# Dense experts for 336 tokens instead of 342: six more tokens go through gathers

## The chip, the cores and the metric

The kernel runs on one core of a Trainium2 chip. The metric is the device time of an execution in microseconds, as the median of the runs. Beside it there is one profiled execution, whose trace is read here. The core has TensorE (PE, matmuls), VectorE (DVE), ScalarE (ACT), GpSimd (POOL) and SyncE (SP), whose queue issues nearly all plain DMAs; GpSimd issues the gathers.

## The reference

One encoder layer on two groups of 256 tokens of width 2048, 512 tokens in all, in fp32. After norm and modulation comes a mixer (retention and differential attention), and then the part that this change is about, a retrieval of experts:

```python
def _peer(h, w_query, sub_keys, u_tab, v_tab):
    def block(xb):                                  # 128 tokens
        q = (xb @ w_query).reshape(TOKEN_BLOCK, PEER_HEADS, 2, PEER_QDIM // 2)
        s = jnp.einsum("nhpd,hpkd->nhpk", q, sub_keys)
        sv, si = lax.top_k(s, PEER_TOPK)            # 16 of 128 keys, twice
        ...                                         # 16 best pairs of 256, per head
        g = jax.nn.softmax(top_s, axis=-1)          # 8 x 16 = 128 slots a token
        hid = jax.nn.gelu(jnp.einsum("nd,ned->ne", xb, u_tab[eidx]))
        return jnp.einsum("ne,ned->nd", g * hid, v_tab[eidx])
```

There are 128 x 128 = 16384 experts, each one row of 2048 in `u_tab` and one in `v_tab`. Each token uses 128 of them. The layer ends with a norm, a gate and the residual.

## The kernel before

The first 1230 us hold the modulation, the projections, the mixer and its output product, and the routing (which 128 experts each token takes, with which gates). The change leaves them nearly as they are. Then two ways of computing the experts run side by side.

**Dense.** For `ND` = 342 of the 512 tokens (tokens 128 to 469) every expert is computed and weighted with a table of gates that is zero where a token does not use an expert. The experts go in 128 blocks of 128. An *up unit* is one block of `u`, 1 MB: 48 matmuls with 128 columns of weights stationary and 342 token columns moving, in fp32 split in a high and a low part (hi x hi and hi x lo on L1096, low x hi on L1103). ScalarE makes the high part of the weights (`raw_hi`, L1504), VectorE the low part (`raw_lo`, L2082); then ScalarE does gelu, VectorE multiplies by the gates (`up_gate`), and the product is split again into `w_hi` and `w_lo`. A *down unit* is 1 MB of `v`, 8 blocks of it by 256 output columns: 48 matmuls (L1157, L1158, L1163) into two PSUM banks, which VectorE adds to `y_t` (`y_add`, L2203). Eight ups and eight downs are a super block; `ORDER` lists all 256 units, unit k in place k. SP loads unit k + 3 once unit k is done, into a ring of three.

**The gate table.** It is made before the dense loop settles, in the *table stage*: for each dense token a product of two one-hot matrices (L1138), in groups of four tokens, between the products of seven up units (`TABLE_UNITS`). VectorE and ScalarE make the one-hots, ScalarE moves the results to a stage buffer of 38 tokens (`table_out`), and SP stores it to DRAM when full. Nine stages make 342. The last one is stored in four quarters, so that the first blocks can be loaded early. In the dense loop SP loads the gates of four blocks at a time (`g_load`) into `g_ring`.

**Gathered.** Token rows 0 to 127 (one per partition, 128 slots each) and the last 42 tokens (*mixed*, three partitions for each token, 43 slots each) fetch only the rows that they use: 171 gathers of u rows, one row of 8 KB for each partition, each followed by a dot product on VectorE (`dot`, L2212) in phase one, and 171 gathers of v rows with a multiply-add into `acc_a` or `acc_x` on VectorE (`accumulate`, L2225) in phase two. The ring has three buffers, and GpSimd issues gather n when dot n - 3 is done. `GATHERS[k]` says which dots VectorE does in its step k, the step in which it also serves units k - 1 and k + 1: phase one at steps 17 to 132, phase two at 137 to 254. At `TURN` the hidden values go through gelu and get their gates. At the end TensorE adds `acc_x` to its 42 tokens by a matmul with the 0/1 matrix `pick_x`.

Order on an engine is the order of the code; semaphores tie the engines.

Of the kernel before, what the change touches and what calls it, by code (L numbers as in the profile page):

```python
# [69 lines left out]
ND = T - P - XT  # L70
# [8 lines left out]
DOTS = SLOTS + XSLOTS  # L79
# [6 lines left out]
STAGE = 38  # L86
# [51 lines left out]

def slot_at(n):
    m, j = n // 4, n % 4  # L140
    return (False, SLOTS + m) if j == 1 else (True, 3 * m + max(j - 1, 0))
# [11 lines left out]
def build_program(nc, x, ct, c_rows, ada_w, ada_wt, ada_b, rows, w_t, w_v, w_o, w_q, keys_t, decay, lams, post1, pre2, post2,  # L153
                  u_t, v_t, u_tab, v_tab, ident_c, dist_c, alibi_c, iota_c, out, mod_d, silu_d, mix_d, g_d, x1_d):
# [8 lines left out]
    with ExitStack() as ctx:  # L163
# [107 lines left out]
        acc_x = placed("acc_x", W0, [P, D])[:, :]  # L271
        h2_hi = rounded("h2_hi", W0 + LOOP, [P, KD, ND])
# [6 lines left out]
        eidx_last = take(SLOTS).bitcast(u32)  # L279
# [17 lines left out]
        stage = [placed(f"stage{n}", a, [P, NKEYS, STAGE]) for n, a in enumerate((M0, at))]  # L297
# [74 lines left out]
        def bank(i):  # L372
            return psum[:, i * NB:(i + 1) * NB]
# [69 lines left out]
        def _(sp):  # L443
# [219 lines left out]
            def stage_store(n, quarters=(0,)):  # L663
                sp.wait_ge(S["g_ev"], PER_STAGE * (n + 1))
                if n < NSTAGE - 1:
                    sp.dma_start(g_d[n], stage[n % 2][:, :, :].rearrange("p i c -> p (i c)")).then_inc(S[f"g_out{n % 2}"], 16)
                    return

                for q in quarters:
                    i = slice(QUARTERS[q], QUARTERS[q + 1])  # L670
                    sp.dma_start(g_d[n, :, i.start * STAGE:i.stop * STAGE], stage[n % 2][:, i, :].rearrange("p i c -> p (i c)"))\
                        .then_inc(S[f"g_quarter{q}"], 16)

            def g_load(q):
# [4 lines left out]
                sp.dma_start(g_ring[:, q % 2, :, :], g_d[:, :, QUAD * q * STAGE:QUAD * (q + 1) * STAGE].rearrange("n j c -> j n c"))\  # L679
# [10 lines left out]
            for a in range(XG):  # L690
# [18 lines left out]
            for k in range(EARLY - 1, UNITS):  # L709
# [1781 lines left out]
```

## Time and profile before

| | us |
|---|---|
| median of 3 runs | 3285.76 (3284.59 to 3288.32) |
| the profiled execution, its own time | 3282.5 |
| its span in the trace | 3280.7 |
| TensorE busy | 3218.1 (98%) |
| VectorE busy | 2664.5 (81%) |
| ScalarE busy | 1044.9 (32%) |
| GpSimd busy | 924.3 (28%) |
| DMA | 914 MB, 279 GB/s over the span |

Busy times of matmuls overlap, since they are pipelined: what a matmul costs is read from the start of one to the start of the next. Idle time of an engine that is not the bottleneck costs nothing. Line numbers are those of the kernel before.

### The profile page before, as it was taken

The numbers are of one execution on the slowest core, as the hardware profiler recorded it, in microseconds if no ns is written. First come the engines' busy times: TensorE is split into PE (matmuls) and PEld (weight loads), VectorE is DVE, ScalarE is ACT, GpSimd is POOL, SyncE is SP. The second block draws the span as 40 slices with busy tenths as digits, with TensorE's granted clock in tenths as the row PEclk, the third lists the DMA queues.
The fourth block names the chain that finished last, engine by engine and source line by source line (L and its number), as shares of the span: only waits on it lengthen the run. The fifth ranks groups of instructions, "written<-read, shape, count | busy, mean of one in ns | idle before, by whom it ended". The sixth has DMA issues, their size and how long they took to land. (4 is left out here: it accounts for less than half of the span.)

```text
span 3280.7 us, 48326 instructions
## 1 busy us (share of the span) xinstructions
PE 3218.1 (98%) x19393; PEld 2969.5 (91%) x19393; DVE 2664.5 (81%) x3913; ACT 1044.9 (32%) x1380; POOL 924.3 (28%) x542
## 2 busy tenths in 40 slices
PE   7999999998999999999999999999999999999998
PEld 3788888888995449999999999999999999999998
DVE  4688888887885769968888888888688888888888
ACT  2222323234222005943323332332332332323332
POOL 2100000003551775013333333333133332343332
PEclk9999999999999999999999999999999999999999
DMA  9845444445556103579999999999799989999987
GB/s 393 310 161 176 161 167 170 169 161 200 204 196 266 72 32 122 223 267 370 348 361 358 356 355 364 354 348 363 292 370 351 361 345 348 356 351 353 360 336 294
DMA packets 174222, 914.05 MB, mean 279 GB/s; under 512 B 16303, under 2 KB 54104, under 8 KB 79832
## 3 DMA queue, kind: packets, MB, share of 16 engines
q1 hardware_dynamic: 124790, 552.84, 45.4%
q0 software_dynamic: 49248, 358.63, 28.0%
q8 instruction: 130, 2.13, 0.3%
q14 instruction: 54, 0.44, 0.0%
HBM read 875.79 MB, written 34.03 MB: 277 GB/s over the span
## 5 line engine op out<-in xcount | busy, mean ns | idle before, releaser
L1504 ACT ACTIVATE sb_raw_hi<-sb_raw_ring 128x2048 fp32r<-128x2048 f32 x256 | 491.0, 1918 | 1144.9 <-DMA sb_raw_ring<-in_v_t 559.6
L2082 DVE TENSOR_TENSOR sb_raw_lo<-sb_raw_ring,sb_raw_hi 128x2048 fp32r<-128x2048 f32 x256 | 586.0, 2289 | 107.5 <-ACT sb_raw_hi L1504 107.1
L1096 PE MATMUL ps_all<-sb_h_hi,sb_raw_hi 128*128 128x342 f32 x2048 | 646.0, 320 | 0.0
L1096 PE MATMUL ps_all<-sb_h_lo,sb_raw_hi 128*128 128x342 f32 x2048 | 645.6, 320 | 0.0
L1157 PE MATMUL ps_all<-sb_w_hi,sb_raw_hi 128*128 128x342 f32 x2032 | 639.7, 319 | 5.1 <-DVE sb_w_lo L2187 3.6
L1158 PE MATMUL ps_all<-sb_w_lo,sb_raw_hi 128*128 128x342 f32 x2032 | 639.0, 320 | 0.0
L2409 POOL DMA_INDIRECT sb_gather_ring<-in_u_tab,sb_kept x171 | 298.6, 1746 | 742.5 <-DVE sb_kept L2212 564.3
L2409 POOL DMA_INDIRECT sb_gather_ring<-in_v_tab,sb_kept x171 | 306.0, 1789 | 615.7 <-DVE sb_acc_a L2225 410.0
L1157 PEld LDWEIGHTS ps_all<-sb_w_hi,sb_raw_hi 128*128 128x128 f32 x2032 | 385.2, 190 | 7.0 <-issue 4.3
L1096 PEld LDWEIGHTS ps_all<-sb_h_lo,sb_raw_hi 128*128 128x128 f32 x2048 | 386.0, 188 | 0.0
L1096 PEld LDWEIGHTS ps_all<-sb_h_hi,sb_raw_hi 128*128 128x128 f32 x2048 | 385.4, 188 | 0.0
L1158 PEld LDWEIGHTS ps_all<-sb_w_lo,sb_raw_hi 128*128 128x128 f32 x2032 | 383.5, 189 | 0.0
L1103 PE MATMUL ps_all<-sb_h_hi,sb_raw_lo 128*128 128x342 f32 x2048 | 352.0, 321 | 0.5 <-DVE sb_raw_lo L2082 0.5
L1163 PE MATMUL ps_all<-sb_w_hi,sb_raw_lo 128*128 128x342 f32 x2032 | 340.2, 319 | 0.0
L1103 PEld LDWEIGHTS ps_all<-sb_h_hi,sb_raw_lo 128*128 128x128 f32 x2048 | 326.0, 189 | 1.0 <-DVE sb_raw_lo L2082 1.0
L1163 PEld LDWEIGHTS ps_all<-sb_w_hi,sb_raw_lo 128*128 128x128 f32 x2032 | 323.8, 188 | 0.0
L2225 DVE SCALAR_TENSOR_TENSOR sb_acc_a<-sb_gather_ring,sb_kept,sb_acc_a 128x2048 f32<-128x2048 f32 x127 | 298.2, 2348 | 12.4 <-DMA sb_gather_ring<-in_v_tab,sb_kept 9.0
L2335 POOL TENSOR_TENSOR sb_w_low<-sb_w_raw,sb_w_high 128x1024 fp32r<-128x1024 f32 (+1 forms) x36 | 92.4, 2594 | 744.9 <-ACT sb_w_high L1433 744.9
L2212 DVE CUSTOM_DVE_ANT_0 sb_gather_ring<-sb_gather_ring,sb_arena 128x2048 f32<-128x2048 f32 x128 | 290.9, 2287 | 2.9 <-DMA sb_gather_ring<-in_u_tab,sb_kept 2.8
L1305 ACT ACTIVATE sb_w_high<-sb_w_raw 128x1536 fp32r<-128x1536 f32 (+1 forms) x62 | 104.9, 1694 | 370.5 <-PE ps_all L773 367.2
L771 PE MATMUL ps_all<-sb_h_hi,sb_w_high 128*128 128x512 f32 x480 | 191.7, 399 | 2.1 <-DVE sb_h_lo L1709 1.7
L772 PE MATMUL ps_all<-sb_h_lo,sb_w_high 128*128 128x512 f32 x480 | 187.1, 390 | 0.0
(325 smaller groups left out, 5268.3 us busy)
## 6 DMA issues: line engine op xcount, KB each, us to landing
sb_raw_ring<-in_u_t SPq DMA_DIRECT2D x128, 1024.0 KB, 6.9
sb_raw_ring<-in_v_t SPq DMA_DIRECT2D x128, 1024.0 KB, 7.2
sb_arena<-in_ada_wt SPq DMA_DIRECT2D x94, 512.0 KB, 6.0
sb_w_raw<-in_w_t SPq DMA_DIRECT2D x32, 1024.0 KB, 4.9
sb_small<-in_ada_w SPq DMA_DIRECT2D x30, 1024.0 KB, 11.2
sb_w_raw<-in_w_v SPq DMA_DIRECT2D x32, 768.0 KB, 4.4
sb_g_ring<-table_scratch SPq DMA_DIRECT2D x32, 684.0 KB, 9.8
table_scratch<-sb_stage SPq DMA_DIRECT2D x8, 2432.0 KB, 8.2
```

Source lines behind the costliest of these rows:

```text
L771: mm(b, a_hi, b_hi, start=start, stop=False)
L772: mm(b, a_hi, b_lo, start=False, stop=False)
L1096: last = mm(acc, raw_hi[:, r[0], kk * P:(kk + 1) * P], part[:, kk, :], start=i == 0, stop=False)
L1103: last = mm(acc, raw_lo[:, place, kk * P:(kk + 1) * P], h2_hi[:, kk, :], start=False, stop=kk == KD - 1)
L1157: mm(accs[c], v, w_hi[:, slots[e], :], start=e == 0, stop=False)
L1158: last = mm(accs[c], v, w_lo[:, slots[e], :], start=False, stop=False)
L1163: last = mm(accs[c], raw_lo[:, place, e * VW + c * P:e * VW + (c + 1) * P], w_hi[:, slots[e], :], start=False, stop=e == S8 - 1)
L1504: acti(raw_hi[:, k % 2, :], raw_ring[:, k % RAW, :], ACT.Copy).then_inc(S["un_hi"], 1)
L2082: vec.tensor_tensor(raw_lo[:, k % RAW, :], raw_ring[:, k % RAW, :], raw_hi[:, k % 2, :].bitcast(f32), ALU.subtract)\
L2212: vec.tensor_tensor_reduce(out=ring, in0=ring, in1=h2a if own else h2x[rows, :], scale=1.0, scalar=0.0, op0=ALU.mult, op1=ALU.add, accum_o ...
L2225: vec.scalar_tensor_tensor(acc, ring, hid_all[rows, c:c + 1], acc, ALU.mult, ALU.add).then_inc(S["gr_used"], 1)
L2409: pool.indirect_dma_start(out=gather_ring[:, n % GRING, :], out_offset=None, in_=u_tab if n < DOTS else v_tab, in_offset=bass.IndirectOffs ...
```

## The change

Six of the dense tokens (464 to 469) become a third kind of gathered token, *few*: 21 partitions for each token, 6 x 21 = 126 partitions, 7 slots in each. That makes 7 gathers more in each phase, 178 for 171. In phase one they come last, in phase two first. `ND` is 336, the table has 8 stages of 42 tokens, and its DRAM tensor is laid out by expert row, group of four blocks, stage and token, so that a `g_load` reads 5376 bytes in a piece, where it read 608; the stores write pieces of 672 bytes, where they wrote whole rows.

The new tokens' normed rows go to DRAM (`few_d`) and come back near the end of phase one, each spread over 21 partitions, into the place of the mixed tokens' rows, and their expert numbers and gates go by way of `route_d`. Their accumulator lies in that same place, and is folded by TensorE at the start of block 10 into 16 x 6 columns, which are copied into `y_last` at the end.

```diff
+XB = 6
+XBP = P // XB
+XBR = XB * XBP
+ND = T - P - XT - XB
+XBSLOTS = -(-SLOTS // XBP)
+DOTS = SLOTS + XSLOTS + XBSLOTS
-STAGE = 38
+STAGE = 42
...
+MIXED, FEW = mixed_columns(), list(range(SLOTS + XSLOTS, DOTS))
+COLUMNS = (MIXED + FEW, FEW + MIXED)
+FOLD_BLOCK = 10
...
+        XE_MIXED = 32 * (XG + 1)
+        XE_ALL = XE_MIXED + 32 * XB * len(FEW_PARTS)
...
-                    sp.dma_start(g_d[n], stage[n % 2][:, :, :].rearrange("p i c -> p (i c)")).then_inc(S[f"g_out{n % 2}"], 16)
+                    sp.dma_start(g_d[:, :, n, :], stage[n % 2][:, :, :].rearrange("p (q i) c -> p q (i c)", i=QUAD))\
+                        .then_inc(S[f"g_out{n % 2}"], 16)
...
-                sp.dma_start(g_ring[:, q % 2, :, :], g_d[:, :, QUAD * q * STAGE:QUAD * (q + 1) * STAGE].rearrange("n j c -> j n c"))\
+                sp.dma_start(g_ring[:, q % 2, :, :], g_d[:, q, :, :])\
                     .then_inc(S[f"g_in{q % 2}"], 16)
...
+            sp.dma_start(route_d[0], eidx_last_f[P - XT - XB:P - XT, :]).then_inc(S["xe_in"], 16)
+            sp.dma_start(route_d[1], gates[P - XT - XB:P - XT, NT - 1, :]).then_inc(S["xe_in"], 16)
             next_load(PRE - 1)
+            sp.wait_ge(S["xe_in"], XE_MIXED)
+            for v, dst in enumerate((eidx_x_f, gates_x)):
+                for j in range(XB):
+                    for first, rows_, columns in FEW_PARTS:
...
+                if k == RELOAD:
+                    sp.wait_ge(S["gr_used"], LAST_MIXED + 1)
+                    for j in range(XB):
+                        sp.dma_start(h2x[j * XBP:(j + 1) * XBP, :], few_d[j:j + 1, :].partition_broadcast(XBP)).then_inc(S["h2x_in"], 16)
...
+            def fold_few():
+
+                pe.wait_ge(S["pick_x"], 1)
+                pe.wait_ge(S["gr_used"], DOTS + XBSLOTS)
+                for k in range(KD):
+                    last = mm(bank(2)[:, k * XB:(k + 1) * XB], acc_few[0:XBR, k * P:(k + 1) * P], pick_few[0:XBR, :], start=True, stop=True)
+                last.then_inc(S["yt_done"], 1)
...
-            act.wait_ge(S["xe_in"], 32 * XG)
+            act.wait_ge(S["xe_in"], XE_MIXED)
             for n in range(NGROUP):
```

SP's queue where the table stage begins, before, from the five weight loads ahead of it to the second stage store (`sb_kept` takes the mixed tokens' expert numbers and gates):

```order
L635 DMA sb_raw_ring<-in_u_t 128x2048 x5
L693 DMA sb_kept<-sb_route_a 42x43
L694 DMA sb_kept<-sb_route_b 42x43
L693 DMA sb_kept<-sb_route_a 42x43
L694 DMA sb_kept<-sb_route_b 42x43
L693 DMA sb_kept<-sb_route_a 42x42
L694 DMA sb_kept<-sb_route_b 42x42
L635 DMA sb_raw_ring<-in_u_t 128x2048
L666 DMA table_scratch<-sb_stage_91 128x4864
L635 DMA sb_raw_ring<-in_u_t 128x2048
```

And with the change, from the last of those copies on:

```order
L732 DMA sb_kept<-sb_route_b 42x42
L733 DMA route_scratch<-sb_route_a 6x128
L734 DMA route_scratch<-sb_route_b 6x128
L671 DMA sb_raw_ring<-in_u_t 128x2048
L741 DMA sb_kept<-route_scratch 18x7
L741 DMA sb_kept<-route_scratch 1x2
...
L741 DMA sb_kept<-route_scratch 1x2
L703 DMA table_scratch<-sb_stage_91 4096x1x168
L671 DMA sb_raw_ring<-in_u_t 128x2048
```

Two writes to DRAM stand behind the six copies, ahead of what ScalarE waits for, and 24 small reads stand between a weight load and the first stage store.

VectorE at the end of the loop, before, from the `memset` of `y_last` to the last addition to `y_t` but one:

```order
L2281 MEMSET sb_y_last 128x16x42
L2203 TENSOR_TENSOR sb_y_t<-ps_all,sb_y_t 128x684
L2082 TENSOR_TENSOR sb_raw_lo<-sb_raw_ring,sb_raw_hi 128x2048
L2225 SCALAR_TENSOR_TENSOR sb_acc_a<-sb_gather_ring,sb_kept,sb_acc_a 128x2048
L2225 SCALAR_TENSOR_TENSOR sb_acc_x<-sb_gather_ring,sb_kept,sb_acc_x 126x2048
...
L2203 TENSOR_TENSOR sb_y_t<-ps_all,sb_y_t 128x684
L2082 TENSOR_TENSOR sb_raw_lo<-sb_raw_ring,sb_raw_hi 128x2048
L2225 SCALAR_TENSOR_TENSOR sb_acc_x<-sb_gather_ring,sb_kept,sb_acc_x 126x2048
L2203 TENSOR_TENSOR sb_y_t<-ps_all,sb_y_t 128x684
L2082 TENSOR_TENSOR sb_raw_lo<-sb_raw_ring,sb_raw_hi 128x2048
L2225 SCALAR_TENSOR_TENSOR sb_acc_a<-sb_gather_ring,sb_kept,sb_acc_a 128x2048
L2203 TENSOR_TENSOR sb_y_t<-ps_all,sb_y_t 128x684
```

And with the change, the last two steps of these:

```order
L2272 TENSOR_TENSOR sb_y_t<-ps_all,sb_y_t 128x672
L2150 TENSOR_TENSOR sb_raw_lo<-sb_raw_ring,sb_raw_hi 128x2048
L2296 SCALAR_TENSOR_TENSOR sb_acc_a<-sb_gather_ring,sb_kept,sb_acc_a 128x2048 x2
L2272 TENSOR_TENSOR sb_y_t<-ps_all,sb_y_t 128x672
L2150 TENSOR_TENSOR sb_raw_lo<-sb_raw_ring,sb_raw_hi 128x2048
L2296 SCALAR_TENSOR_TENSOR sb_acc_a<-sb_gather_ring,sb_kept,sb_acc_a 128x2048
L2272 TENSOR_TENSOR sb_y_t<-ps_all,sb_y_t 128x672
```

The last step but one has two accumulates where it had one.

TensorE at the fold, with the change, between the last down unit of block 9 and the first up unit of block 10 (`sb_h2x` holds the few tokens' sums):

```order
L1211 MATMUL ps_all<-sb_w_lo,sb_raw_hi 128x336
L1216 MATMUL ps_all<-sb_w_hi,sb_raw_lo 128x336 x16
L1290 MATMUL ps_all<-sb_kept,sb_h2x 128x6 x16
L1149 MATMUL ps_all<-sb_h_hi,sb_raw_hi 128x336
L1149 MATMUL ps_all<-sb_h_lo,sb_raw_hi 128x336
```

Before, the row of 128x6 is not there, and the others have 342 columns.

## Rows read from the trace of the kernel before

**Rows 1.** Busy time by stretch: length, busy us (instructions), PEclk, DMA share, GB/s.

```profile
1438.30:1442.00 3.70, 3.67 (x13) 3.70 (x14) 2.29 (x1) 0.85 (x1) 3.40 (x2) 0.50 1.07 373
1442.00:1446.00 4.00, 4.00 (x23) 4.00 (x22) 0.00 (x0) 0.00 (x0) 1.24 (x2) 0.80 1.02 425
1800.00:2100.00 300.00, 300.00 (x1912) 300.00 (x1911) 250.29 (x216) 92.06 (x79) 104.58 (x60) 1.00 0.93 356
```

**Rows 2.** The page's memory traffic in 40 equal slices of 82 us.

```profile
GB/s 393 310 161 176 161 167 170 169 161 200 204 196 266 72 32 122 223 267 370 348 361 358 356 355 364 354 348 363 292 370 351 361 345 348 356 351 353 360 336 294
```

**Rows 3.** What TensorE waited for: us in total, times, longest us.

```profile
PE ps_all L1157 <- DVE sb_w_lo L2187: 3.6, 1, 3.6
PE ps_all L1138 <- DVE sb_hot L2166: 3.1, 7, 1.2
PE ps_all L1157 <- ACT sb_raw_hi L1504: 1.2, 3, 0.5
```

**Rows 4.** The page's costliest groups: operands, xcount | busy, mean ns | idle.

```profile
L1096 PE MATMUL ps_all<-sb_h_hi,sb_raw_hi 128*128 128x342 f32 x2048 | 646.0, 320 | 0.0
L1157 PE MATMUL ps_all<-sb_w_hi,sb_raw_hi 128*128 128x342 f32 x2032 | 639.7, 319 | 5.1 <-DVE sb_w_lo L2187 3.6
L2225 DVE SCALAR_TENSOR_TENSOR sb_acc_a<-sb_gather_ring,sb_kept,sb_acc_a 128x2048 f32<-128x2048 f32 x127 | 298.2, 2348 | 12.4 <-DMA sb_gather_ring<-in_v_tab,sb_kept 9.0
```

**Rows 5.** Timeline of TensorE, ends of three unbroken runs: start us, us, what.

```profile
879.74 0.28 PE L772 MATMUL ps_all<-sb_w_low,sb_mix_hi 128*128 128x256 f32 x1
...
899.90 0.28 PE L772 MATMUL ps_all<-sb_w_low,sb_mix_hi 128*128 128x256 f32 x1
...
499.67 0.33 PE L771 MATMUL ps_all<-sb_w_high,sb_h_hi 128*128 128x384 f32 x1
...
509.38 0.34 PE L773 MATMUL ps_all<-sb_w_high,sb_h_lo 128*128 128x384 f32 x1
...
549.93 0.40 PE L772 MATMUL ps_all<-sb_h_lo,sb_w_high 128*128 128x512 f32 x1
...
560.36 0.40 PE L773 MATMUL ps_all<-sb_h_hi,sb_w_low 128*128 128x512 f32 x1
```

**Rows 6.** Timeline of TensorE where the first down unit begins.

```profile
1438.75 0.49 PE L1158 MATMUL ps_all<-sb_w_lo,sb_raw_hi 128*128 128x342 f32 x1
...
1443.31 0.46 PE L1158 MATMUL ps_all<-sb_w_lo,sb_raw_hi 128*128 128x342 f32 x1
```

**Rows 7.** Timelines where the table stage begins: SP's queue, ScalarE, TensorE.

```profile
1283.81 0.75 SPq L694 DMA_DIRECT2D sb_kept<-sb_route_b  x1
...
1301.75 0.33 SPq L666 DMA_DIRECT2D table_scratch<-sb_stage  x1
...
1286.94 0.40 ACT L1562 ACTIVATE sb_hot<-sb_iota,sb_by_slot 128x128 f32<-128x128 f32 x1 [3.00 <-DMA sb_kept<-sb_route_b]
...
1288.01 1.13 PE L1138 MATMUL ps_all<-sb_hot 128*128 128x128 f32 x8 [1.46 <-ACT sb_hot L1564]
```

**Rows 8.** TensorE's table products: ns min/median/max, first and last start.

```profile
L1138 PE MATMUL ps_all<-sb_hot x684: 270/275/378, 1283.4 to 1418.7; 128*128 128x128 f32 x171
```

**Rows 9.** Timelines between table stage and first down unit: SP's queue, VectorE.

```profile
1425.80 1.05 SPq L679 DMA_DIRECT2D sb_g_ring<-table_scratch  x2
...
1430.29 1.79 DVE L2183 TENSOR_TENSOR sb_acc_a<-sb_acc_a,sb_g_ring 128x342 f32<-128x342 f32 x4 [1.13 <-DMA sb_g_ring<-table_scratch]
```

**Rows 10.** Timeline of TensorE: the nearest rows to a matmul of six columns.

```profile
27.96 1.05 PE L758 MATMUL ps_all<-sb_tiny,sb_tops 128*128 128x2 f32 x8 [0.73 <-ACT sb_tops L1272]
```

**Rows 11.** Gathers, line 2409: time from issue to landing.

```profile
DMA to landing us min/median/max: 5.5/9.2/14.1
```

**Rows 12.** Timeline of VectorE at the end of the program.

```profile
3251.52 2.35 DVE L2225 SCALAR_TENSOR_TENSOR sb_acc_a<-sb_gather_ring,sb_kept,sb_acc_a 128x2048 f32<-128x2048 f32 x1
...
3259.86 1.22 DVE L2241 TENSOR_TENSOR sb_raw_ring<-ps_all,sb_gate_sb 128x1024 f32<-128x1024 f32 x1
...
3261.98 0.87 DVE L2203 TENSOR_TENSOR sb_y_t<-ps_all,sb_y_t 128x684 f32<-128x684 f32 x1 [0.90 <-PE ps_all L1163]
```

More of the change, by code:

```diff
@@ L136, in slot_of, with mixed_columns, kind_of @@
     return slots_of(b // S8 % 3)[b % S8]
+def mixed_columns():
+    at = {1 + 15 * m // 4: SLOTS + m for m in range(XSLOTS)}
+    own = iter(range(SLOTS))
+    return [at[n] if n in at else next(own) for n in range(SLOTS + XSLOTS)]
+MIXED, FEW = mixed_columns(), list(range(SLOTS + XSLOTS, DOTS))
+COLUMNS = (MIXED + FEW, FEW + MIXED)
+LAST_MIXED = max(n for n in range(DOTS) if SLOTS <= COLUMNS[0][n] < SLOTS + XSLOTS)
+RELOAD = DOT0 + LAST_MIXED * (TURN - 1 - DOT0) // DOTS + 2
+FOLD_BLOCK = 10
+FOLDED = 1 + 2 * S8 * FOLD_BLOCK + 3
+def kind_of(c):
+    return "own" if c < SLOTS else "mixed" if c < SLOTS + XSLOTS else "few"
 def slot_at(n):
-    m, j = n // 4, n % 4
-    return (False, SLOTS + m) if j == 1 else (True, 3 * m + max(j - 1, 0))
+    c = COLUMNS[n // DOTS][n % DOTS]
+    return kind_of(c), c
 def full_groups(n):
@@ L271, in build_program @@
         acc_x = placed("acc_x", W0, [P, D])[:, :]
+        acc_few = h2x
+        acc_of = {"own": (acc_a, P), "mixed": (acc_x, XP), "few": (acc_few, XBR)}
         h2_hi = rounded("h2_hi", W0 + LOOP, [P, KD, ND])
@@ L296, in build_program @@
         early_w = placed("early_w", at + WR, [P, S8 + 2, ND])
-        stage = [placed(f"stage{n}", a, [P, NKEYS, STAGE]) for n, a in enumerate((M0, at))]
+        stage = [placed(f"stage{n}", a, [P, NKEYS, STAGE]) for n, a in enumerate((at, M0))]
         pick_x = placed("pick_x", at + 2 * WR, [P, P])[:, :]
@@ L1606, in _ @@
                     acti(hid_all[:, 0:SLOTS], hid_all[:, 0:SLOTS], ACT.Gelu)
-                    acti(hid_all[0:XP, SLOTS:DOTS], hid_all[0:XP, SLOTS:DOTS], ACT.Gelu).then_inc(S["hid_gelu"], 1)
+                    for rows_, c in ((XP, slice(SLOTS, SLOTS + XSLOTS)), (XBR, slice(SLOTS + XSLOTS, DOTS))):
+                        last = acti(hid_all[0:rows_, c], hid_all[0:rows_, c], ACT.Gelu)
+                    last.then_inc(S["hid_gelu"], 1)
+                if k == FOLDED:
+                    act.wait_ge(S["yt_done"], 1)
+                    acti(y_few, bank(2)[:, 0:KD * XB].rearrange("p (k j) -> p k j", k=KD), ACT.Copy).then_inc(S["y_last"], 1)
             def y_square(t, half):
                 i = 2 * t - 2 + half
-                act.wait_ge(S["yt_done"], i + 1)
+                act.wait_ge(S["yt_done"], i + 2)
                 c = slice(half * PIECE, (half + 1) * PIECE)
```

85 lines of the change are left out of this document (55 added, 30 removed).

## The prediction

> **What bounds the kernel now.** I read the busy time by stretch first. In the dense stage (about 1440 to 3260 us) TensorE is busy without a gap: 300 us of 300, 1912 matmul records, at the full clock, 1.00, of its two levels, 2.4 GHz [rows 1]. That is 300 / 1912 = 156.9 ns from one matmul of 342 columns to the next. VectorE is busy 250 us of the same 300, the DMA engines 0.93 of it, moving 356 GB/s. Then the waits: of 3280.7 us TensorE waited 3.6 us for the first down unit's `w_lo`, 3.1 us in the table stage and 1.2 us for `raw_hi` [rows 3]. So the time of the dense stage is the number of matmuls times their spacing, and a term counts if it changes either, or if it makes TensorE wait at one of four places: the start of the table stage, the first down unit, a ring that runs late, the tail.
>
> **The narrower matmul.** There are 2048 matmuls on each of three operand pairs of the up units and 2032 on each of three of the down units, as the two rows shown of the six [rows 4], and 48 on the lines of the last block's first down unit, L1186 to L1190: 12288. Seven units (336 matmuls) run inside the table stage and go with it below; 11952 are left. All go from 342 to 336 columns. What six columns are worth comes from the spacing of other widths in this trace, each in a run without a gap. At 256 columns it is 168 matmuls from 879.74 to 899.90 us, 120.0 ns; at 384, 56 matmuls from 499.67 to 509.38, 173.4 ns; at 512, 46 matmuls from 549.93 to 560.36, 226.7 ns [rows 5]. These lie on one line: 53.4 ns for each 128 columns, 0.417 ns a column, and 13.3 ns beside it. The line gives 155.9 ns at 342 columns, but the row gives 156.9: this width pays 1.0 ns that the three others don't. 342 is the only one of the four widths that isn't a multiple of 16, and 336 is one; whether the extra goes with that, no row shows. So the saving is 6 x 0.417 = 2.5 ns a matmul if it stays and 3.5 ns if it goes: 29.9 to 41.8 us. I take 3.2 ns, nearer to the line, since three widths of three lie on it: **38.2 us saved**.
>
> The trace also shows what a lower clock does: with the clock granted at 0.50 (1.2 GHz) [rows 1], the matmuls from 1438.75 to 1443.31 us, 16 spacings, are 285.0 ns apart [rows 6], which is 342 / 1.2 and nothing beside it. The Trainium skill says the same in "TensorE: Matmul & The Clock Gate", section "Wait — 56ns, not 53.3ns?": columns over 1.2 GHz when slow, columns over 2.4 GHz plus a constant when fast. By that rule the 13.3 ns is a constant and nothing is special about 342, so it makes the saving 2.5 ns and the sum 8.3 us later than mine; the 1.0 ns off the line speaks against it, and its constant, about 2.5 ns, is not what these rows show.
>
> **Seven more gathers a phase.** They bring 7 dots and 7 accumulates on VectorE, at 2.35 us for an accumulate [rows 4] and near the same for a dot: 33 us in all, against 50 us idle per 300 us. Per unit VectorE has 178/116 = 1.53 instead of 171/116 = 1.47 of them in phase one. The busy share goes from 0.83 to about 0.88 as the unit shrinks from 7.53 to 7.38 us. Hidden by VectorE's idle time; without that cover it would be the whole 33 us. A gather lands 9.2 us after issue (14.1 at worst) [rows 11], and its ring of three gives it three dots' time, 3 x 4.8 = 14.4 us less one dot. Where two steps with two dots now stand in a row (eight times in phase one, never before) the gap is only some 7.4 us, so VectorE waits 2 us there, and catches up in the next step with one dot. Taken at 0, 0 to +8.
>
> **The fold.** TensorE gets 16 fp32 matmuls of six columns at the start of block 10. The nearest rows are the 128x2 matmuls: 8 records in 1.05 us, some 0.10 us each, two records a matmul [rows 10]. 32 records make **+3.2 us**, 1.6 if both passes overlap, 4.2 if each takes what the first does. Its inputs (accumulates placed some 20 units earlier) are long ready, so it waits for nothing. The copies that follow (ScalarE, VectorE, one DMA) are small and beside it.
>
> **The start of the table stage.** ScalarE waited 3.00 us here for the last copies of route data, and TensorE 1.46 us for ScalarE [rows 7]. The change puts two more DMAs, writes to DRAM, in front of that wait, each at 0.75 us of issue as the one at 1283.81: 1.5 us later. VectorE, which paces the stage, gets its banks later by the same. I take **+1.3 us**, 0.5 if the write lands faster than the copies do, +6 if the longer idle lets the clock fall as it did after 3.6 us at the first down unit. Behind it SP issues 24 small DMAs, 8 to 18 us of queue (0.33 to 0.75 us each), past a unit load whose data is due 40 us later and the first stage store, which was issued at 1301.75 and would now go at 1297 to 1307; ScalarE needs it landed two stages after the start, near 1320. Hidden; nothing.
>
> **The table stage.** It takes 1283.4 to 1418.7 us for 342 tokens [rows 8], 0.396 us each; six fewer make 2.4 us, its share of narrow matmuls included. 88 groups instead of 90, but the half groups cost more per token: **-2.0 us**, -3 to 0.
>
> **The first down unit.** TensorE waited 3.6 us: the stage's first quarter is stored, the two `g_ring` loads go out at 1425.80, VectorE's first gate follows at 1430.29 after waiting for them [rows 9]. Each load was 9 x 128 pieces of 608 B, and is 128 of 5376 B; the store becomes 512 pieces of 672 B for 128 of 2432 B. I give the loads back 1.5 us of their 4.5, the store takes 0.4 more, and the units ahead, shorter by 0.3 us, put TensorE there sooner. Wait 2.8 us, and a little less slow clock behind it: **-1.3 us**. Ends: -6 (no wait, and the 17 slow matmuls at 285 instead of 157 ns gone), +1.
>
> **The tail.** The last step but one has two accumulates instead of one, 2.35 us later on VectorE. Its idle before the last `y` addition is 0.90 us [rows 12]; the rest, **+1.5 us**, reaches the turns, squares and outputs. 0 to +3.
>
> Sum: -38.2 + 3.2 + 1.3 - 2.0 - 1.3 + 1.5 = **-35.5 us**. The profiled execution took 3282.5 us, giving 3247.0; the median of the runs, 3285.76, is 3.3 us above it, giving 3250.3. I say **3249 us**.
>
> **Rivals.**
> *The extra 1.0 ns stays* (2.5 ns a matmul): 8.3 us less saved, **3257 us**. For it: a per-matmul cost needn't know the width. Against: three widths on a line.
> *The DMA engines become the bound.* A unit moves 1.049 MB of weights, 1.474 gathers of 1.049 MB and an eighth of a 0.70 MB gate load, 2.68 MB in 7.53 us, which is the 356 GB/s of the row. After: 2.74 MB in 7.38 us, 372 GB/s. If 356 were the limit, a unit would take 7.70 us, 0.17 more than now, over 234 units with gathers: +40 us where 38 were to be saved, with the small terms about nothing: **3325 us**, slower. It decides from the point where unit loads land so late that ScalarE's `raw_hi` comes after TensorE asks. For it: 0.93 busy. Against: the 356 is just TensorE's demand, slices of 82 us reach 370 GB/s in the dense stage and 393 at the start [rows 2], 4 us reached 425 [rows 1], and some 34000 pieces of 608 B leave the stage (the small pieces are now the table stage's stores). The Trainium skill, "DMA: Bandwidth & Descriptors", section "Specifications", sets about 358 GB/s for a core's HBM traffic; by that rule the rival would come out at 3316 us. The trace doesn't agree: 370 and 393 are above it [rows 2].
> *VectorE falls behind* at the doubled steps and TensorE waits a unit's `w_lo` or bank now and then, 1 us at ten places: **3259 us**.
> *The table stage stalls* on its own stores: 4096 pieces of 672 B a stage. The g_ring loads moved 2304 pieces in 4.5 us, so 8 us of the 16.6 there are. If they took 20, six stages pay 3.5 us: **3270 us**.
> That the change doesn't do what it says has no room: widths and counts are in the program's order.
>
> **How the numbers follow.** Forecast 0.58, extra stays 0.24, VectorE 0.05, stores 0.06, DMA bound 0.07. The likeliest one's own range, with its bounds, is 3238 to 3260. 8 in 10 takes in the second and third and most of the fourth: **3237 to 3268**. What measurement tells from no change is 0.2%, 6.6 us, so faster is below 3279: 0.58 + 0.24 + 0.05 + most of 0.06, set down a little: 0.90. Slower by as much is the DMA case: 0.07. Same: 0.03.
>
> **What would show it.** Right: 153.3 to 153.7 ns a matmul (1953 or so in 300 us), TensorE still 300 of 300, VectorE near 265, DMA near 370 GB/s, the wait for `w_lo` at the first down unit under 3.6 us, the ScalarE wait at the table stage 4 to 5 us, 16 matmuls of six columns in about 3 us. Wrong: 154.4 ns (the extra stayed), TensorE waits for `raw_hi` or `raw_lo` through the dense stage with a DMA behind them, or a table stage longer than 136 us.

## The result

| | before | after |
|---|---|---|
| median of 4 runs each, on one chip, us | 3286.86 (3284.59 to 3288.32) | 3265.84 (3264.57 to 3270.59) |
| the profiled execution, its own time | 3282.5 | 3265.75 |
| its span | 3280.7 | 3263.6 |

The ratio is 0.9938, with a 95% interval of 0.9923 to 0.9953: faster by 0.6%, 21 us. The profiled executions differ by 16.75 us. The forecast was 3249 us, from a gain of 35.5 us, in a range of 3237 to 3268. The sign and the range held, the second by 2 us. Of the gain 21 us came, 16.75 in the profiled executions.

### The profile page after: what moved, and what is told of

The parts are those of the page before. It is cut to its first block and busy times, and to the rows that moved or that the text cites. A ratio compares the mean times of both kernels' runs of the same rounds, so it can differ in the third digit from the quotient of the medians.

```text
span 3263.6 us, 48433 instructions
## 1 busy us (share of the span) xinstructions
PE 3184.7 (98%) x19413; PEld 2936.4 (90%) x19413; DVE 2689.8 (82%) x3930; ACT 1039.4 (32%) x1378; POOL 899.1 (28%) x556
## 5 line engine op out<-in xcount | busy, mean ns | idle before, releaser
L1210 PE MATMUL ps_all<-sb_w_hi,sb_raw_hi 128*128 128x336 f32 x2032 | 627.5, 318 | 19.2 <-ACT sb_raw_hi L1567 15.8
L1149 PE MATMUL ps_all<-sb_h_hi,sb_raw_hi 128*128 128x336 f32 x2048 | 637.4, 318 | 0.0
L1149 PE MATMUL ps_all<-sb_h_lo,sb_raw_hi 128*128 128x336 f32 x2048 | 637.2, 318 | 0.0
L1211 PE MATMUL ps_all<-sb_w_lo,sb_raw_hi 128*128 128x336 f32 x2032 | 626.6, 317 | 0.0
L2486 POOL DMA_INDIRECT sb_gather_ring<-in_u_tab,sb_kept x178 | 283.0, 1590 | 754.3 <-DVE sb_kept L2283 584.9
L2486 POOL DMA_INDIRECT sb_gather_ring<-in_v_tab,sb_kept x178 | 296.7, 1667 | 610.7 <-DVE sb_acc_a L2296 376.0
L1156 PE MATMUL ps_all<-sb_h_hi,sb_raw_lo 128*128 128x336 f32 x2048 | 342.9, 317 | 1.1 <-DVE sb_raw_lo L2150 1.0
L1216 PE MATMUL ps_all<-sb_w_hi,sb_raw_lo 128*128 128x336 f32 x2032 | 333.7, 316 | 0.0
L1156 PEld LDWEIGHTS ps_all<-sb_h_hi,sb_raw_lo 128*128 128x128 f32 x2048 | 319.2, 188 | 1.6 <-DVE sb_raw_lo L2150 1.6
L1216 PEld LDWEIGHTS ps_all<-sb_w_hi,sb_raw_lo 128*128 128x128 f32 x2032 | 316.8, 188 | 0.0
```

Of the source, the lines that this page charges most:

```text
L1149: last = mm(acc, raw_hi[:, r[0], kk * P:(kk + 1) * P], part[:, kk, :], start=i == 0, stop=False)
L1156: last = mm(acc, raw_lo[:, place, kk * P:(kk + 1) * P], h2_hi[:, kk, :], start=False, stop=kk == KD - 1)
L1210: mm(accs[c], v, w_hi[:, slots[e], :], start=e == 0, stop=False)
L1211: last = mm(accs[c], v, w_lo[:, slots[e], :], start=False, stop=False)
L1216: last = mm(accs[c], raw_lo[:, place, e * VW + c * P:e * VW + (c + 1) * P], w_hi[:, slots[e], :], start=False, stop=e == S8 - 1)
L2486: pool.indirect_dma_start(out=gather_ring[:, n % GRING, :], out_offset=None, in_=u_tab if n < DOTS else v_tab, in_offset=bass.IndirectOffs ...
```

## The profile after

First the busy time by stretch (length, busy us of PE, PEld, DVE, ACT and POOL with their instructions, PEclk, DMA share, GB/s), the row that answers to the last of [rows 1], and the page's traffic in 40 slices, which answers to [rows 2]:

```profile
1800.00:2100.00 300.00, 300.00 (x1952) 300.00 (x1951) 262.39 (x226) 97.01 (x86) 91.54 (x61) 1.00 0.96 372
...
GB/s 386 313 168 175 163 164 176 155 177 201 194 193 284 65 39 79 235 265 377 367 375 374 365 380 377 368 374 319 296 379 374 354 369 361 374 364 359 378 361 308
```

300 / 1952 = 153.7 ns from matmul to matmul (156.9 before), VectorE 262 us of 300, 372 GB/s: the steady state is what was forecast. Now TensorE's waits (us in total, times, longest), the rows that answer to [rows 3]:

```profile
PE ps_all L1210 <- ACT sb_raw_hi L1567: 15.8, 3, 12.4
...
PE ps_all L1191 <- ACT sb_hot L1627: 3.2, 2, 1.9
...
PE ps_all L1210 <- DVE sb_w_lo L2256: 2.7, 1, 2.7
...
PE ps_all L1227 <- DVE sb_y_t L2272: 2.0, 1, 2.0
...
PE ps_all L1191 <- DVE sb_hot L2234: 1.4, 3, 0.5
```

The wait for `raw_hi` has grown from 1.2 to 15.8 us, and 12.4 of it is one wait. The timelines of SP's queue, ScalarE and TensorE (start us, duration, what, idle before and its end) show where:

```profile
2232.13 2.03 SPq L766 DMA_DIRECT2D sb_h2x<-few_scratch  x6
2239.12 0.36 SPq L671 DMA_DIRECT2D sb_raw_ring<-in_v_t  x1
...
2264.21 1.91 ACT L1567 ACTIVATE sb_raw_hi<-sb_raw_ring 128x2048 fp32r<-128x2048 f32 x1 [21.70 <-DMA sb_raw_ring<-in_v_t]
...
2266.17 0.65 PE L1210 MATMUL ps_all<-sb_w_hi,sb_raw_hi 128*128 128x336 f32 x1 [12.38 <-ACT sb_raw_hi L1567]
```

This is the reload: six copies of 168 KB, each of which puts one row of `few_d` into 21 partitions of `h2x`. The unit load that SP issues 7 us behind them lands 25 us after its issue, at 2264.19, so late that ScalarE idles 21.7 us and TensorE 12.4. The DMA engines over 2225 to 2275 us, in 40 slices of 1.25 us (busy tenths, GB/s):

```profile
DMA  9999999999989999999999999999999844440099
GB/s 413 406 415 419 433 426 419 406 426 426 387 275 308 269 269 301 301 243 288 216 229 223 282 229 256 288 321 413 419 419 426 374 203 184 184 177 13 0 197 393
```

From 2239 us on they are as busy as ever and move 216 to 321 GB/s instead of 387 to 433, for 20 us; then, near 2266 us, four slices run at full speed on four tenths of the engines (184 GB/s). The stretches around:

```profile
2240.00:2260.00 20.00, 13.79 (x91) 13.51 (x89) 9.62 (x9) 1.92 (x1) 2.80 (x3) 0.96 1.02 277
2260.00:2280.00 20.00, 13.83 (x73) 13.83 (x74) 13.85 (x11) 5.74 (x3) 4.52 (x3) 0.70 0.63 242
2534.00:2538.00 4.00, 4.00 (x37) 4.00 (x35) 3.51 (x3) 1.91 (x1) 2.94 (x2) 1.00 0.62 217
2538.00:2542.00 4.00, 4.00 (x17) 4.00 (x18) 3.01 (x2) 0.00 (x0) 0.72 (x1) 0.57 1.01 428
```

In the second row the granted clock is down to 0.70: after the wait, some 20 matmuls came at the lower of the two levels, 280 ns apart, 2.8 us more; 12.5 + 2.8 is **15.3 us** for the reload. The last two rows are the fold at the start of block 10 and what follows: TensorE has no gap there, but behind its tiny matmuls the clock is 0.57 for 4 us. The fold's own row (ns min/median/max, first and last start) and the second place with a new wait, near the first down unit:

```profile
L1290 PE MATMUL ps_all<-sb_kept,sb_h2x x32: 171/254/254, 2534.6 to 2538.0; 126*128 126x6 f32 x32
```
```profile
1425.45 9.55 SPq L709 DMA_DIRECT2D table_scratch<-sb_stage  x3
1435.05 2.67 SPq L717 DMA_DIRECT2D sb_g_ring<-table_scratch  x1
1437.76 0.45 SPq L671 DMA_DIRECT2D sb_raw_ring<-in_v_t  x1
...
1435.13 0.39 PE L1210 MATMUL ps_all<-sb_w_hi,sb_raw_hi 128*128 128x336 f32 x1 [2.71 <-DVE sb_w_lo L2256]
...
1454.92 0.42 PE L1210 MATMUL ps_all<-sb_w_hi,sb_raw_hi 128*128 128x336 f32 x1 [3.29 <-ACT sb_raw_hi L1567]
```

The first down unit starts at 1435.13 (1438.33 before) after 2.71 us of waiting (3.64 before), but two units on there are 3.3 us of waiting, with slow matmuls behind, 5.1 us together, which before had not.

## The experiments

Ratios are to the kernel before on the same chip; their intervals are about 0.0015 either way, 5 us (from 0.0009 to 0.0025). Smaller differences are read from the traces, by two numbers for each. The *loss* is the time from the first product of the first down unit to the first transposition of `y_t`, which holds 240 units of 48 matmuls, less 11520 times the spacing of that kernel (156.9 ns for the two kernels of 342 columns, 154.2 for the kernel of 336 of 342, 153.7 for the others). The last column is the part of it that falls at the reload: the time between 2230 and 2300 us beyond what its matmuls take at the steady spacing. Both come from one profiled execution each, and a kernel's executions differ by up to 20 us, so the table sets its own time beside the median of its runs: a loss from a profile 9 us below the median, as that of the eight copies, is too small for its kernel. The kernels without the reload, with other rows in it (*own rows*, 126, 128 and 16 rows) and the two narrow ones leave work out or compute with other data; only their times are read.

| kernel | ratio (interval) | profiled / median, us | first down unit, us | first transposition, us | loss, us | at the reload, us |
|---|---|---|---|---|---|---|
| before | 1 | 3282.50 / 3286.86 | 1438.33 | 3252.95 | 7.1 | 0 |
| after | 0.9938 (0.9923 to 0.9953) | 3265.75 / 3265.84 | 1435.13 | 3234.87 | 29.1 | 15.1 |
| no reload | 0.9894 (0.9880 to 0.9908) | 3248.63 / 3251.84 | 1434.73 | 3218.97 | 13.6 | 0 |
| reload in one copy of 126, few rows | 0.9939 (0.9926 to 0.9953) | 3262.21 / 3266.67 | 1435.63 | 3232.54 | 26.3 | 9.1 |
| reload in six copies, rows of their own | 0.9950 (0.9937 to 0.9964) | 3274.60 / 3274.07 | 1438.54 | 3244.39 | 35.2 | 18.6 |
| reload spread over six units | 0.9904 (0.9891 to 0.9917) | 3260.32 / 3257.42 | 1435.00 | 3230.57 | 25.0 | 2.6 |
| reload in one copy of 126 rows | 0.9927 (0.9914 to 0.9941) | 3261.11 / 3261.00 | 1436.26 | 3231.37 | 24.5 | 4.7 |
| reload in one copy of 128 rows | 0.9904 (0.9884 to 0.9924) | 3255.12 / 3253.84 | 1440.11 | 3224.49 | 13.8 | 0 |
| reload in eight copies of 16 rows | 0.9938 (0.9924 to 0.9951) | 3254.37 / 3262.99 | 1436.40 | 3224.55 | 17.5 | 5.5 |
| before, 336 dense tokens alone | 0.9898 (0.9878 to 0.9918) | 3255.98 / 3251.84 | 1435.32 | 3226.61 | 20.7 | 0 |
| before, 336 of 342 columns | 0.9938 (0.9913 to 0.9962) | 3269.39 / 3263.60 | 1438.61 | 3239.94 | 24.9 | 0 |
| after, old layout of the table | 0.9978 (0.9966 to 0.9991) | 3275.00 / 3277.29 | 1436.42 | 3245.34 | 38.3 | 18.4 |
| before, new layout of the table | 1.0012 (1.0003 to 1.0021) | 3290.60 / 3288.94 | 1444.90 | 3261.05 | 8.7 | 0 |
| reload by way of 128 rows, fold spread | 0.9925 (0.9911 to 0.9938) | 3258.09 / 3258.09 | 1439.95 | 3228.40 | 17.8 | 0 |

**What the reload costs.** The theory was that it holds up the load behind it.

```diff
-                if k == RELOAD:
-                    sp.wait_ge(S["gr_used"], LAST_MIXED + 1)
-                    for j in range(XB):
-                        sp.dma_start(h2x[j * XBP:(j + 1) * XBP, :], few_d[j:j + 1, :].partition_broadcast(XBP))...
```

> The changed kernel without the six copies that reload h2x at unit 121; the dots of the six tokens then multiply by the rows that h2x held before, which costs the same time. Theory A (the reload holds up the unit load behind it): the 21.7 us wait of ScalarE for sb_raw_ring and the 12.4 us wait of TensorE for sb_raw_hi near 2264 us go, and with them the slow matmuls behind, so 15 us: about 3250.5 us. Rival B (the transfers of that stretch are late anyway, since the gathers fill the queues): the wait moves by a few us only, 3260 to 3266 us.

The wait is gone, the loss falls by 15.5 us and the ratio by 0.0044, 14.5 us. (Another wait for `raw_hi`, 4.2 us at the second unit behind the first down unit, stays as in after.) Theory A holds: the reload is worth nearly all that the forecast missed.

**Why it costs so much.** Three theories: the six copies lie on a part of the DMA queues and pile up there (1); any burst of 1 MB ahead of a load costs this (2); many reads of one row in DRAM are slow (3). Three edits of the same lines:

```diff
+ one copy:     sp.dma_start(h2x[0:XBR, :], few_d.unsqueeze(1).broadcast_to([XB, XBP, D]))
+ own rows:     sp.dma_start(h2x[j * XBP:(j + 1) * XBP, :], x1_d[j * XBP:(j + 1) * XBP, :])     # six times
+ spread:       if RELOAD <= k < RELOAD + XB: ...                                               # copy k - RELOAD alone
```

> The reload as one DMA over 126 partitions from the same six rows, each read 21 times. Theory 1 (a copy into 21 partitions lies on a part of the 16 queues, and six of them pile up on the same ones): a single copy is spread evenly, it adds 1 MB / 0.37 MB per us = 2.8 us of transfers, the wait of TensorE falls from 12.4 us to 0 to 3 us: 3251 to 3255 us. Theory 2 (1 MB in a burst ahead of a load) and theory 3 (one DRAM row read by all is slow): no change, 3263 to 3267 us.

> The reload still as six DMAs of 21 partitions, but each partition reads a row of its own (of x1_scratch: other data, so the dots of the six tokens are of other vectors). Theory 3 (many reads of one DRAM row are slow): the wait of TensorE falls to 0 to 3 us, 3251 to 3255 us. Theories 1 and 2 (uneven queues, burst): no change, 3263 to 3267 us.

> The six DMAs of the reload go out one per unit, behind the loads of units 124 to 129, instead of all behind that of 124. Theory 2 (the burst): 168 KB is 0.45 us at 372 GB/s, the loads have over 3 us to spare at each unit, so the wait goes: 3251 to 3254 us. Theory 1 (uneven queues): each copy delays its own queues by 21 rows on 7 queues = 3 x 0.31 = about 1 us, hidden as well, 3251 to 3254 us. Theory 3 (slow row): every copy is as slow as before but apart from the others, so the waits are small and repeated, 3254 to 3262 us.

Rows of their own made it no better (TensorE waited 15.9 us): theory 3 is out. One copy of 126 partitions still cost a wait of 6.5 us, 9.1 us with the slow matmuls behind it, and its median of 3266.67 us did not fall below that of after: it came out where theories 2 and 3 had put it, and theory 1 by itself is not enough. Spread over six units the copies cost no wait above 1.7 us and 2.6 us in all; this version was 0.9904 against 0.9938. Its 3257.42 us miss the 3251 to 3254 of theories 1 and 2. The loss of 25.0 is from the slowest but one of its five runs (3260.32 us; they go from 3251 to 3260), and 13 us of it lie behind 2300 us, 7 at the fold and the rest in small gaps, whose cause stays open.

**126 or 128 partitions.** In the slow cases all 16 engines are busy at some 270 GB/s: 0.49 us for 8 KB on each, where 420 GB/s are 0.31. So it isn't only that some queues are longer than others. Theory 4 is that a copy whose partitions are not the 128 of a load is dealt to the queues in another way than the loads, and slows the packets of all. The next kernels differ by two rows.

```diff
+ 126:   sp.dma_start(h2x[0:XBR, :], x1_d[0:XBR, :])
+ 128:   sp.dma_start(h2x, x1_d[0:P, :])
+ 8x16:  sp.dma_start(h2x[j * 16:(j + 1) * 16, :], x1_d[j * 16:(j + 1) * 16, :])     # eight times
```

> The reload as one DMA into all 128 partitions, from 128 rows of x1_scratch (other data for the six tokens' dots). Six copies of 21 partitions and one of 126 both slowed every packet from 0.31 to 0.5 us for over 12 us. Theory 4 (126 or 21 partitions are dealt to the queues unlike the 128 of a load, so that queues write each other's partitions): packets stay at 0.31 us, the rate at 400 GB/s, TensorE waits 0 to 3 us: 3252 to 3256 us. Theory 2 (any burst of 1 MB just there): as the copy over 126, TensorE waits about 6.5 us, 3262 to 3268 us.

> As the run with one copy of 128 rows of x1_scratch, but 126 rows: two rows fewer, the same source, place and moment. Theory 4 (a copy whose partitions are not all 128 is dealt to the queues unlike the loads and the gathers, and slows all packets): rate 190 to 300 GB/s for over 10 us, TensorE waits 5 to 8 us, 3261 to 3267 us. Rival (it was the broadcast from few rows that was slow in the one-copy run, and the six pieces in the other): packets at full speed, 3252 to 3256 us.

> The reload as eight copies of 16 partitions (rows of x1_scratch), 128 in all. If it is the number of partitions over the whole that matters, or that pieces start at a multiple of 16: full speed, 3252 to 3256 us. If every copy of less than 128 partitions is dealt unevenly, as the 21 of each in the changed kernel: TensorE waits about 12 to 16 us, 3264 to 3274 us.

The same 50 us and 40 slices of the DMA engines as above, first for 128 rows in one copy:

```profile
DMA  9999999999999999999999999898999989999998
GB/s 433 426 419 438 419 415 419 439 419 419 419 426 419 426 374 387 406 419 419 426 433 419 393 387 367 334 380 301 328 301 387 334 315 426 360 419 419 426 400 360
```

then for 126 rows in one copy:

```profile
DMA  9999999999999999999999999999999999899598
GB/s 419 413 433 410 427 421 440 413 419 426 426 426 413 413 315 288 315 282 262 256 229 275 315 419 419 419 419 419 419 426 419 419 400 374 262 341 400 138 380 367
```

and for eight copies of 16:

```profile
DMA  9999999999999999999999999999478958989989
GB/s 441 413 430 426 433 433 419 334 210 203 229 243 288 360 406 374 419 419 426 426 426 419 419 419 426 419 413 387 157 131 321 393 118 367 380 236 426 315 321 413
```

With 128 rows the rate stays at 374 to 439 GB/s for 30 us (single slices fall to 301 later), TensorE does not wait, and the loss is that of the kernel without a reload, 13.8 against 13.6. With two rows fewer it sinks to 229 to 315 for nine slices, 11 us, all engines busy. The load behind it is late, TensorE waits 3.1 us, where 5 to 8 were expected, and 4.7 us go in all. The rest of that kernel's loss of 24.5 is not at the reload, and by the runs' times alone the two kernels are not told apart: their intervals overlap. Eight pieces of 16 sink the rate to 203 to 288 for five slices, 6 us, and cost 5.5 us. There TensorE waited for VectorE and not for a load:

```profile
PE ps_all L1210 <- DVE sb_y_t L2272: 4.0, 1, 4.0
```

VectorE had itself waited 4.5 and 2.7 us for two late gathers, in front of the addition to `y_t` that frees the bank. The profile is that kernel's fastest execution; its median, 3262.99 us, lies in neither of the two ranges of the expectation, and nearer to the upper one. So theory 4 holds by the rates and waits of the traces, and its rival form failed: it is not enough that pieces start at a multiple of 16, or that they make 128 in all. Theory 2 stands for nothing by itself: a burst of 1 MB costs nothing here if it is laid out as the loads are. One copy of 126 partitions cost 9.1 us from six rows and 4.7 from 126 rows; whether the source adds something, one execution of each does not decide.

The Trainium skill, "DMA: Bandwidth & Descriptors", section "Why a DMA increments its semaphore by 16 and not by 1", says that a DMA uses the largest number of engines up to 16 that divides the slowest dimension of both its sides, and one that SP issues the lowest-numbered of them: by that 16 of 16 for 128 rows, 14 for 126 rows and 7 for 21. The trace of after agrees: the four slices with 0.4 of the engines and 184 GB/s are 7 of 16, at the rate of the full set (7/16 x 415 = 182). The section "The descriptor swizzle" says that in a copy of 128 partitions each engine writes one port of the SBUF. My guess from both, which the page does not state, is that 14 engines with nine rows each, or 16 with one row each of eight copies, write other engines' ports while the loads and gathers keep to their own, and that this is why packets on all queues took half as long again. The rates of the four shapes agree with it; no run here shows a port.

**What the narrower matmuls give alone.** Two edits of the kernel before, in short:

```diff
-ND = T - P - XT
+ND = T - P - XT - 6
-STAGE = 38
+STAGE = 42
-enumerate((M0, at))
+enumerate((at, M0))
```

> The kernel before with 336 dense tokens and 8 table stages of 42, and nothing in place of the six tokens (their experts are left out). If the terms of the sum for the matmuls (-38.2 us) and the table stage (-2) are right, 3286.9 - 40 = 3247 us, and what the changed kernel has above that (19 us) is the price of the six tokens' way: reload 15, fold 5. If the narrow matmuls give less than was summed (for example since another engine sets the pace at times), 3255 to 3265 us, and the reload's price would have been found in another place than the sum says.

```diff
+MMW = ND - 6
-acc = bank(r[1])[:, 0:ND]
+acc = bank(r[1])[:, 0:MMW]        # and so every operand of the expert matmuls
```

> The kernel before with every expert matmul on 336 of its 342 columns; the layout of the operands, the table stage and all other engines' work stay (the last six columns are left out of the products). Theory A (the time of a matmul goes with its columns, and the 1.0 ns that 342 columns take above the line goes with the number): 300 us hold 1952 matmuls, 153.7 ns apart, and the time is 3286.9 - 38 = 3249 us. Rival B (the 1.0 ns come from rows that start 342 elements apart): 154.4 ns apart at the least, 3257 us. Rival C (elementwise work on 342 columns holds the matmuls at 156.9 ns in part): over 3260 us.

The first gave 0.9898, 33.5 us, of the 40 summed: a median of 3251.84 us, between the two values expected. Its table stage and spacing are as summed; the loss is 20.7 us instead of 7.1, with no reload and no fold in it, in a profile 4 us above the median. TensorE's waits there, the first row of them in the dense stage:

```profile
PE ps_all L1158 <- ACT sb_raw_hi L1505: 8.5, 6, 2.8
```

Six waits for late loads, none longer than 2.8 us, where before had three in 1.2 us. The second, with all other work as before, gave half of what A said, 0.9938, 20 us; its median of 3263.60 us lies in the range of rival C. Its spacing, from the stretch 1900 to 2100 us:

```profile
1900.00:2100.00 200.00, 200.00 (x1297) 200.00 (x1297) 169.83 (x147) 62.92 (x53) 71.64 (x40) 1.00 0.93 360
```

That is 154.2 ns: 2.7 of the 3.2 ns go with the six columns, and 0.5 only in kernels whose rows lie 336 apart (0.6 if after is counted in the same stretch, 1302 matmuls). The first of these two kernels is at 153.7 ns too, with the old table in DRAM, so it isn't that table; but the work of VectorE and ScalarE on 342 columns is still there in the second, and was not taken apart from the rows' distance. So B's effect may be there, small, and C's can't be more than it. The time was lost otherwise, in late loads: the loss is 24.9 us (about 19, if the profile stood at its kernel's median). None of the rivals had that. Both kernels share what after has not: the old layout of the gate table. The kernel without the reload, which has the new layout, lost 1.4 us between 1480 and 3205 us besides its fold; the first of these two lost 15.9 there.

**The layout of the gate table.** It is undone in the changed kernel, and done alone in the one before.

```diff
-sp.dma_start(g_ring[:, q % 2, :, :], g_d[:, q, :, :])
+sp.dma_start(g_ring[:, q % 2, :, :], g_d[:, :, QUAD * q * STAGE:QUAD * (q + 1) * STAGE].rearrange("n j c -> j n c"))
 # and both stores as in the kernel before; the second experiment is the reverse
```

> The changed kernel with the gate table in DRAM laid out as before (a stage's rows together, the loads in eight pieces of 672 bytes to a partition). SyncE then issues the last three quarter stores in 1.5 us in place of 9.6, and the loads behind them go out on time: if the 3.3 us wait of TensorE near 1449 us and the slow matmuls behind it come from these stores, they go, -5 us. Against it, each load of four columns of the table again moves 1024 small packets; if these cost loads their time once the gathers fill the queues, ScalarE's waits for sb_raw_ring grow. I expect 3262 to 3266 us (the first, -5, in part given back), and the 12.4 us wait of TensorE at the reload to stay; above 3270 us the layout would be worth more than its stores cost.

> The kernel before with the new layout of the gate table alone (342 columns, 9 stages of 38). Before loses nothing to late loads behind 1445 us, since its loads have 7.53 us each. Theory A (the layout pays only where the loads are near their limit): 3285 to 3289 us, no change. Rival B (the small packets of the old layout slow every stretch): 3275 to 3280 us. SyncE issues the last quarter stores in over 8 us in place of 1.4; if that costs what it seemed to in the changed kernel, TensorE waits 3 us more near 1450 us: 3290 us.

With the old layout the changed kernel has the ratio 0.9978 instead of 0.9938, 13 us, and a loss of 38.3 instead of 29.1. I had expected 3262 to 3266 us and the median is 3277.29: wrong, and by the bound set ahead (above 3270) the layout is worth more than its stores cost. TensorE's first row of waits there:

```profile
PE ps_all L1210 <- ACT sb_raw_hi L1567: 21.1, 5, 15.9
```

The reload's wait is 15.9 instead of 12.4, 3.3 us more with the slow matmuls, and single short ones are added before and after. At the old pace the layout gives nothing, theory A: loss 8.7 against 7.1. In that kernel's profile the table stage is 5 us longer and the first down unit starts 6.6 us later; by the runs it is slower by 0.12%, 4 us. So 1024 pieces of 672 bytes for a load instead of 128 of 5376 cost something at 7.38 us for a unit and 2.7 MB to move, and nothing in the dense stage at 7.53 us. That it is the margin of the loads that makes the difference is argued from these two pairs, and from the kernel of 336 tokens alone. The steady rate shows nothing of it, since TensorE is busy all through most of these stretches; a load that is late once is not made up.

It also settles SyncE's share. With the old layout SP issued the three quarter stores in 1.41 us, not 9.55:

```profile
1427.49 1.41 SPq L709 DMA_DIRECT2D table_scratch<-sb_stage  x3
...
1454.99 0.43 PE L1210 MATMUL ps_all<-sb_w_hi,sb_raw_hi 128*128 128x336 f32 x1 [2.35 <-ACT sb_raw_hi L1567]
```

and TensorE still waited 2.35 us at the same unit, 4.2 with the slow matmuls. The reading that the blocked queue makes that wait falls; at most 1 us of it can be that. What remains is that loads of units and gates, stores and the first gathers all start there; which of them decides stays open.

**A version with the reload mended.** The six rows are written out to 128 rows of a DRAM scratch during the table stage, and the fold's products stand between those of a unit.

```diff
+                if n == 2 * PER_STAGE:
+                    for j in range(XB):
+                        sp.dma_start(rows_d[j * XBP:(j + 1) * XBP, :], few_d[j:j + 1, :].partition_broadcast(XBP))...
+                    sp.dma_start(rows_d[XBR:P, :], few_d[0:P - XBR, :])...
...
+                    sp.dma_start(h2x, rows_d).then_inc(S["h2x_in"], 16)
...
                 for i in range(3 * KD):
                     up_product(k, b, i, place, r)
+                    if fold and i % 3 == 2:
+                        fold_few(i // 3)
```

> The changed kernel with two edits: the six rows are spread over 128 rows of a scratch in DRAM during the table stage (seven copies from DRAM to DRAM where TensorE does not wait for loads), and the reload is one copy of these 128 rows; and the 16 products of the fold stand one behind each third product of a unit in place of all in a row. The first takes away the 12.4 us wait and the slow products behind it, 15.3 us, less the 2 to 3 us that a 1 MB copy costs where it is dealt evenly; the second takes the 1.6 us of slow clock behind the fold, and keeps its 3 us. Together 3265.8 - 15 = 3251 us (3247 to 3254). If the copies in DRAM hold up the table stage, the first down unit starts later than 1435 us and the time is up to 5 us longer.

At the reload TensorE does not wait at all, and behind the fold the clock stays up:

```profile
2524.00:2528.00 4.00, 4.00 (x32) 4.00 (x30) 2.32 (x2) 1.59 (x1) 3.31 (x2) 1.00 0.84 305
...
2536.00:2540.00 4.00, 4.00 (x28) 4.00 (x27) 4.00 (x3) 0.48 (x1) 0.00 (x0) 1.00 0.93 334
```

The loss falls from 29.1 to 17.8, where 15 us had been summed: 15.1 us at the reload and 1.6 behind the fold went, and over 5 us of gaps came in elsewhere behind 2300 us, whose cause stays open. And the copies in DRAM cost the table stage 5 us, the upper case of the expectation; SP took 11 us to issue six of them, and in that time TensorE stood still once, for nothing that the trace names:

```profile
1344.41 2.05 PE L1197 MATMUL ps_all<-sb_hot 128*128 128x128 f32 x8 [4.94 <-issue]
...
1321.08 11.21 SPq L750 DMA_DIRECT2D rows_scratch<-few_scratch  x6
```

The median is 3258.09 us, not 3251. The ratio is 0.9925 (0.9911 to 0.9938), which the measurement does not tell from after's. The plain spreading of the six copies, 0.9904, is the best of the versions that compute everything; its interval lies just below after's.

## Why the prediction was right, and where it fell short

- *The narrower matmul*, -38.2: right. 153.7 ns in [rows 1]'s successor row, within 153.3 to 153.7. The 1.0 ns off the line went in part: 0.2 with the columns, 0.5 with the rows' distance or the work beside it; 0.4 stays above the line's 153.3.
- *Seven more gathers*, taken at 0: right, TensorE never waited for them. VectorE had 262 us of 300 (265 said), and waited 78 us for gathers in all, where before it had waited 15. They land in 5.7/9.4/17.3 us, 5.5/9.2/14.1 before.
- *The fold*, +3.2: the products took 3.5 us (2534.58 to 2538.07), and the clock behind them 1.6 more; the bounds, 1.6 to 4.2, had no slow clock in them. Spread over a unit they cost the same 3.5 us, without the 1.6.
- *"The copies that follow (ScalarE, VectorE, one DMA) are small and beside it."* This sentence speaks of the fold's copies; the reload, the six copies ahead of the few tokens' dots, is in no sentence of the sum. **This is the step that failed**: an edit that was not priced. It cost 15.3 us in the profiled execution, by the ratios of both kernels 14.5, each of which is uncertain by some 5 us. Counting every DMA that SP issues in the loop would have found it, and the number 21 would then have asked which engines carry it.
- *The start of the table stage*, +1.3: the first table product came 0.66 us later (1284.09 for 1283.43), ScalarE's wait was 3.61 for 3.00. The two writes took 0.29 us each to issue, not 0.75.
- *The table stage*, -2.0: from the first table product to the first product behind the last one, 136.0 us became 133.4, -2.6. The stores never stalled it: that rival is out, at stages of 42.
- *The first down unit*, -1.3: the wait fell by 0.9 and the slow clock behind by 0.8, as said; the unit behind lost 5.1 us. With it the term is +3.4. The step that was missing is the next unit's load.
- *The tail*, +1.5: the wait for `y_t` before the last turns is 1.96 us, 0.75 before: +1.2.

By these rows 15.3 + 1.9 + 4.7 of time not forecast, less 1.5 forecast but not lost, make 20.4; the profiled execution came 18.75 us above its own forecast of 3247.0, so 1.7 us are not accounted for.

That the range held is in part luck. The 3265.84 us lie 2 us under its upper bound, in the part that was added for the rivals (the likeliest case by itself ended at 3260), and none of these rivals is what took the time: the wide range covered a cost that it was not made for.

*DMA bound*: as put, false; 372 GB/s over 300 us with TensorE at 300 of 300, in slices to 380. The Trainium skill, "DMA: Bandwidth & Descriptors", section "Specifications", sets about 358; the trace disagrees again. But its point of decision, loads so late that `raw_hi` comes after TensorE asks, was reached now and then. The limit is met in single loads, not in the mean: the reload, and 9 us by the loss or 13 by the ratio if the table is laid out as before. The change's new layout was given 1.5 us at one place in the sum; it was worth about ten, since without it the narrower matmuls would have given part of their gain back. A sum that asked only what the edits cost, and not what the old parts would cost at the new pace, could not show that. *VectorE falls behind*: not seen in after, where the late gathers that it waited for held nobody; in the kernel with eight copies two of them held TensorE for 4 us.

## What to carry to other kernels

List every DMA that a change adds, with its row count, and give each the load behind it: here copies of 21, 16 or 126 partitions in between transfers of 128 made all packets take half as long again for 6 to 20 us, and cost TensorE 5 to 19 us, where one of 128 cost nothing. When a change makes the engine that sets the pace faster, the margin of what feeds it shrinks everywhere, and a thing that cost nothing (small pieces in a load) starts to cost. A mean rate and a busy share do not show that; the longest waits do.

## What the runs showed of the hardware

- Copies into 126 or 21 partitions, or eight of 16, took the DMA rate from about 420 down to between 200 and 320 GB/s with all engines busy; one of 128 left it at 374 to 439.
- Sixteen fp32 matmuls of six columns in a row (32 records in 3.4 us, from 2534.6 to 2538.0), without any gap, were followed by a clock of 0.57. With three wide matmuls between each two of them it stayed 1.00.
- A wait of 2.71 us at 1435.13 was followed by a brief slow part, 1.56 us lost (2.39 after 3.64 us before). It does not go by the length of the wait alone: at the same place a wait of 2.93 us was followed by a clock of 0.50 from 1436 to 1440 us (reload spread), and one of 2.89 us by 1.00 (no reload). At the lower level a matmul of 336 columns took 280 ns, 336 / 1.2 and nothing beside it.
- SP needed 9.55 us to issue three stores of 672-byte pieces, and 1.41 us for the same bytes in long rows.
- Matmuls of 336 columns came 154.2 ns apart where the operand's rows lie 342 elements apart and VectorE and ScalarE work on 342 columns, and 153.7 where both are 336; which of the two makes the 0.5 ns was not tested.
